# Prompt halves of the first two up tiles ahead of the sample part, and every later output-projection tile one sample later

## The reference

```
h = rms_norm(x, g_norm_mix) * (1 + scale_m) + shift_m
mla_t, dsa_t = mixer_projections(h, pos, lw)
o_mla, o_dsa = attend(mla_t, dsa_t)          # samples read 16 pages of 128 cached rows each
x = x + gate_m * (concat(rms_norm(o_mla, g_a), rms_norm(o_dsa, g_b)) @ w_out)
h = rms_norm(x, g_norm_ffn) * (1 + scale_f) + shift_f
g, u = split(h @ w_ffn_in, 2)
x = x + gate_f * ((silu(g) * u) @ w_ffn_out)
```

## Time and profile before

| | us |
|---|---|
| median of 3 runs | 1254.75 |
| lowest, highest | 1250.54, 1258.36 |
| the profiled execution, its time | 1252.33 |
| its span, first to last instruction | 1250.5 |
| PE busy | 1184.0 |
| DVE busy | 675.5 |
| ACT busy | 396.9 |

### The profile page before, as it was taken

How to read it: one execution, slowest core, us unless ns; L and a number is a source line. 1 busy time by engine, 2 the same in 40 slices (tenths; PEclk the granted TensorE clock), 3 DMA queues, 4 the chain that set the end, 5 groups by cost and what they waited for, 6 DMA issues and landing times.

```text
span 1250.5 us, 22534 instructions
## 1 busy us (share of the span) xinstructions
PE 1184.0 (95%) x9176; PEld 1060.3 (85%) x9176; DVE 675.5 (54%) x1508; ACT 396.9 (32%) x772; POOL 92.5 (7%) x138
## 2 busy tenths in 40 slices
PE   6699999998999999999999999989999999979997
PEld 4588896465687899999999888879999999959997
DVE  0643853745888787778867342342433343294330
ACT  3322333532577655555555123311001011000001
POOL 2000002001105300000000121000000000000000
PEclk9799999987999999999999999659999999999999
DMA  9597651022001202222232565302332323133321
GB/s 323 133 281 201 192 170 52 1 68 73 29 17 61 77 1 77 77 77 77 77 127 85 193 207 208 135 1 85 96 89 85 99 84 100 57 93 93 93 69 68
DMA packets 137739, 129.10 MB, mean 103 GB/s; under 512 B 17110, under 2 KB 131171, under 8 KB 135580
## 3 DMA queue, kind: packets, MB, share of 16 engines
q1 hardware_dynamic: 133596, 86.89, 23.5%
q0 software_dynamic: 4064, 41.11, 9.0%
HBM read 124.58 MB, written 3.41 MB: 102 GB/s over the span
## 4 chain that ended last, share of the span: by engine, by line
PE 82%; DVE 9%; DMA 3%; ACT 3%; issue 2%; SPq 0%; POOL 0%; DVEq 0%; ACTq 0%
PE psV L1166 19%; PE psV L950 13%; PE psA L1166 10%; PE psA L687 7%; PE psV L1062 4%; PE psV L887 2%; PE psA L1045 2%; PE psA L1113 2%; PE psA L930 2%; PE psV L911 2%; PE psV L643 2%; PE psV L749 2%; PE psA L1000 1%; PE psA L898 1%; PE psA L1036 1%
## 5 line engine op out<-in xcount | busy, mean ns | idle before, releaser
L950 PE MATMUL psV<-r_r,wide_r 128*128 128x260 f32 x1536 | 207.5, 288 | 3.3 <-DVE msk L1987 2.7
L950 PEld LDWEIGHTS psV<-r_r,wide_r 128*128 128x128 f32 x1536 | 190.4, 189 | 5.9 <-issue 3.3
L1445 ACT ACTIVATE wring<-psV 128x512 f32<-128x512 f32 x128 | 76.1, 596 | 91.5 <-PE psV L950 69.1
L1166 PE MATMUL psV<-qiz_r,wring_r 128*128 128x260 f32 x528 | 93.9, 283 | 0.0
L2183 DVE TENSOR_TENSOR wide<-wide,psV 128x520 f32 (+1 forms) x22 | 15.3, 696 | 138.4 <-PE psV L1166 138.4
L1988 DVE TENSOR_REDUCE msk<-wring 128x8 f32<-128x512 f32 x128 | 86.4, 675 | 0.0
L687 PE MATMUL psA<-wide_r,wring_r 128*128 128x260 f32 x432 | 79.8, 289 | 6.5 <-DVE hT_r L2225 6.4
L1166 PEld LDWEIGHTS psV<-qiz_r,wring_r 128*128 128x128 f32 x528 | 76.2, 188 | 0.0
L1166 PE MATMUL psA<-qiz_r,r_r 128*128 128x260 f32 x352 | 71.7, 285 | 1.6 <-DVE hT_r L2120 1.6
L1166 PE MATMUL psA<-hT_r,r_r 128*128 128x260 f32 x352 | 71.5, 285 | 0.0
L1166 PE MATMUL psA<-qiz_r,wring_r 128*128 128x260 f32 x352 | 71.4, 285 | 0.0
(11 more groups left out here) (490 smaller groups left out, 2600.2 us busy)
## 6 DMA issues: line engine op xcount, KB each, us to landing
wring<-w_ffn_in SPq DMA_DIRECT2D x44, 512.0 KB, 3.8
wide<-w_ada SPq DMA_DIRECT2D x11, 1024.0 KB, 6.8
wring<-w_ffn_out SPq DMA_DIRECT2D x16, 704.0 KB, 4.7
tok<-w_ada SPq DMA_DIRECT2D x9, 1024.0 KB, 7.6
wring<-w_in SPq DMA_DIRECT2D x24, 256.0 KB, 3.4
wring<-w_out SPq DMA_DIRECT2D x8, 512.0 KB, 8.4
wide<-w_out SPq DMA_DIRECT2D x2, 2048.0 KB, 8.3
wring<-w_in SPq DMA_DIRECT2D x20, 128.0 KB, 2.7
```

The lines of the kernel that those rows point to most:

```text
L950: mm = pe.matmul(kx[m % 2][:, hf, :], w, wtab[:, b % 2, l, 2 * k + hf, :], start=(k == 0 and w is high and l == 0), stop=(k == 1 and w is ...
L1166: mm = pe.matmul(out[:, hf, 0:HT], w[:, k, :], x[:, hf * HT:(hf + 1) * HT], start=(k0 + k == 0 and x is xh and w is high), stop=(k0 + k == ...
L1445: A(sq2[m % 2].rearrange("p (x n) -> p x n", x=2), kx[m % 2][:, :, 0:256], ACT.Square).then_inc(kx_squared, 1)
```

## The change

On PE, tile 2 moves from the open stretch to sample 1, tiles 3 to 7 to samples 2 to 6, and the sums of squares to sample 7. The first half of `sample_out` moves from ahead of `weigh_values(7)` to behind `values_out(7)`. The first two up tiles (slots 1 and 3) are split first and made in two parts: the 512 prompt columns (260 and 252) right behind `sample_out(1)`, around the small sum that the samples' DVE steps need, and the 8 sample columns when these are ready. The first two gate tiles follow whole. ACT and DVE follow: squares one sample later, the root at the start of step 6, its reciprocal inside step 7 between `row_sums` and `normalise`, all of `modulate_prompt` after step 7. DVE splits all four tiles of the first turn before the feed-forward. The two tiny matmuls go; counts are raised instead. `spm`, where `sample_out` adds up, moves to another bank.

```diff
-        spm = psA[:, 1, 1, 160:288].rearrange("p (m g b) -> p m g b", m=8, g=2)
+        spm = psA[:, 1, 0, 0:128].rearrange("p (m g b) -> p m g b", m=8, g=2)
...
+            def up_prompt(x, k0, k1):
+
+                s = 2 * x + 1
+                if k0 == 0:
+                    pe.wait_ge(w_split, 9 + x)
+                    pe.wait_ge(v_free, V_U + x - 1)
+                for k in range(k0, k1):
+                    pe.wait_ge(x_split, KD + k + 1)
+                    high, low = pieces(whigh[s])[:, k, :], pieces(wlow[s])[:, k, :]
+                    for w, xx in ((high, xhigh), (high, xlow), (low, xhigh)):
+                        for hf, c, n in ((0, 0, HT), (1, HT, SEQ - HT)):
+                            pe.matmul(sv(V_U + x)[:, hf, 0:n], w, xx[:, k, c:c + n], start=(k == 0 and w is high and xx is xhigh),
+                                      stop=(k == KD - 1 and w is low), skip_group_check=True)
+
             k_scores(0, tile=0)
             weigh(NB - 1)
-            for t in (1, 2):
-                for c4 in range(4):
-                    out_tile(t, c4)
+            for c4 in range(4):
+                out_tile(1, c4)
             pe.wait_ge(lat_out, NB)
             latent_out(NB - 1).then_inc(ol_full, 1)
-            k_scores(1, tile=3)
+            k_scores(1, tile=2)
             for b in range(NB):
                 if b >= 1:
                     values_out(b - 1)
-                if b == NB - 1:
-                    pe.wait_ge(ol_taken, 2)
-                    pe.wait_ge(wo_loaded[0], 16)
-                    for m in range(KD):
-                        sample_out(0, m)
                 weigh_values(b)
                 if b + 2 < NB:
-                    k_scores(b + 2, tile=b + 4 if b < 4 else None, sums=b == 4)
+                    k_scores(b + 2, tile=b + 3 if b < 5 else None, sums=b == 5)
...
             values_out(NB - 1)
+            pe.wait_ge(ol_taken, 2)
+            pe.wait_ge(wo_loaded[0], 16)
+            for m in range(KD):
+                sample_out(0, m)
...
             mm.then_inc(od_full, 1)
+            up_prompt(0, 0, 6)
             pe.wait_ge(s_summed, 1)
-            pe.matmul(ssum_ffn, ones, sum8, start=True, stop=True, skip_group_check=True).then_inc(a_full, 1)
+            pe.matmul(ssum_ffn, ones, sum8, start=True, stop=True, skip_group_check=True).then_inc(a_full, 1 + PADA)
+            up_prompt(0, 6, 8)
+            up_prompt(1, 0, 8)
...
             pe.wait_ge(x_split, 2 * KD + 1)
-            ffn_turn(0)
+            for x in range(2):
+                for k in range(KD):
+                    high, low = pieces(whigh[2 * x + 1])[:, k, :], pieces(wlow[2 * x + 1])[:, k, :]
+                    for w, xx in ((high, xhigh), (high, xlow), (low, xhigh)):
+                        mm = pe.matmul(sv(V_U + x)[:, 1, SEQ - HT:HT], w, xx[:, k, SEQ:T], start=(k == 0 and w is high and xx is xhigh),
+                                       stop=(k == KD - 1 and w is low), skip_group_check=True)
+                mm.then_inc(v_full, 1)
+            for x in range(2):
+                pe.wait_ge(w_split, 11 + x)
+                pe.wait_ge(a_free, A_G + x - 1)
+                passes(pieces(wlow[2 * x]), pieces(whigh[2 * x]), proj, sa(A_G + x)).then_inc(a_full, 1)
             with pe.Fori(1, KF // 2) as i:
...
             for b in range(NB - 1):
+                if b == 6:
+                    prompt_root()
                 take(NB + b)
-                if b == 5:
-                    prompt_root()
...
             A(stat[0:1, 0, 2:3], epsc[0:1], ACT.Sqrt)
-            high_part(1)
-            high_part(2)
+            high_part(0)
             take(2 * NB - 1)
...
-                elif b <= 5:
-                    add_prompt(v, b + 2)
-                elif b == NB - 1:
-                    modulate_prompt(v, 0)
+                elif b <= 6:
+                    add_prompt(v, b + 1)
                 shift(NB + b)
...
-                elif b <= 5:
-                    split_tile(v, 2, b - 4)
+                elif b == 5:
+                    split_first(v, 1, 8)
+                elif b == 6:
+                    split_first(v, 3, 9)
                 elif b == NB - 1:
-                    modulate_prompt(v, 2)
+                    v.wait_ge(v_free, V_SS2 + 1 + PADV)
+                    link(v.reciprocal(root2, root2))
                 normalise(NB + b)
...
                 if b == 6:
-                    v.wait_ge(v_free, V_SS2 + 1)
-                    link(v.reciprocal(root2, root2))
-            modulate_prompt(v, 3)
-            modulate_prompt(v, 4)
+                    split_first(v, 0, 10)
+                    split_first(v, 2, 11)
+            for k in range(3):
+                modulate_prompt(v, k)
             v.wait_ge(od_full, 1)
...
+        def split_first(v, s, n):
+
+            split(v, wraw[s], wlow[s], whigh[s], tail_w[s], 48, n)
...
-            def gate_turn(i, ahead):
+            def gate_turn(i, ahead, first=0):
 
                 for s in range(2):
-                    if s == 0 or ahead:
+                    if s >= first and (s == 0 or ahead):
...
-            with v.Fori(0, KF // 2 - 1) as i:
+            gate_turn(0, True, 1)
+            with v.Fori(1, KF // 2 - 1) as i:
```

More of the change, by code:

```diff
@@ L1074, in prompt_sums @@
                 if c4 == 3:
-                    mm.then_inc(v_full, 1)
+                    mm.then_inc(v_full, 1 + PADV)
             def k_scores(b, tile=None, sums=False):
@@ L1171, in pe_tail @@
             proj = lambda k: (xhigh[:, k, :], xlow[:, k, :])
[L1173 to L1178, removed]
             def ffn_turn(i, need=None):
@@ L1513, in prompt_root @@
             def prompt_root():
-                act.wait_ge(v_full, V_SS2 + 1)
+                act.wait_ge(v_full, V_SS2 + 1 + PADV)
                 act.wait_ge(v_free, V_SS2)
-                A(root2, psV[:, 1, 0, :], ACT.Sqrt, scale=1.0 / D, bias=epsc[:]).then_inc(v_free, 1)
+                A(root2, psV[:, 1, 0, :], ACT.Sqrt, scale=1.0 / D, bias=epsc[:]).then_inc(v_free, 1 + PADV)
             def high_part(k):
@@ L1534, in act_decode @@
             for b in range(NB - 1):
+                if b == 6:
+                    prompt_root()
                 take(NB + b)
-                if b == 5:
-                    prompt_root()
                 if b + 2 < NB:
                     take_keys(4 * b + 8)
-                else:
-                    high_part(0)
                 exps(NB + b + 1)
@@ L1544, in act_decode @@
                     take_keys(4 * b + 9)
-                if b == 4:
+                if b == 5:
                     prompt_square(6)
@@ L1550, in act_decode @@
                     take_keys(4 * b + 11)
-                if 1 <= b <= 3:
-                    prompt_square(2 * b - 2)
-                    prompt_square(2 * b - 1)
+                if 2 <= b <= 4:
+                    prompt_square(2 * b - 4)
+                    prompt_square(2 * b - 3)
             A(stat[0:1, 0, 2:3], epsc[0:1], ACT.Sqrt)
-            high_part(1)
-            high_part(2)
+            high_part(0)
             take(2 * NB - 1)
-            for k in range(3, 7):
+            for k in range(1, 6):
                 high_part(k)
+            high_part(6)
+            high_part(7)
             act.wait_ge(a_full, A_MIX + 1)
             A(rms8.rearrange("p g b -> p (g b)"), ssum_mix, ACT.Sqrt, scale=1.0 / 512, bias=epsc[:]).then_inc(a_free, 1)
-            high_part(7)
-            act.wait_ge(a_full, A_SS2 + 1)
-            A(root8, ssum_ffn, ACT.Sqrt, scale=1.0 / D, bias=epsc[:]).then_inc(a_free, 1)
+            act.wait_ge(a_full, A_SS2 + 1 + PADA)
+            A(root8, ssum_ffn, ACT.Sqrt, scale=1.0 / D, bias=epsc[:]).then_inc(a_free, 1 + PADA)
         def act_tail(act):
             A = nc.scalar.activation
-            if PADA:
-                act.wait_ge(a_full, A_SS2 + 2)
-                A(stat[0:1, 0, 0:1], sa(A_SS2 + 1)[0:1, 0, 0:1], ACT.Identity).then_inc(a_free, 1)
             with act.Fori(0, KF // 2) as i:
@@ L2080, in dve_decode @@
                 if b == 0:
-                    add_prompt(v, 2)
                     v.wait_ge(ol_full, 1)
@@ L2097, in dve_decode @@
             v.tensor_reduce(sums2[:, 1, :], sq64[:, 4:8].rearrange("p k b -> p b k"), AXX, ALU.add).then_inc(mix_s, 1)
-            modulate_prompt(v, 5)
-            modulate_prompt(v, 6)
+            for k in range(3, 8):
+                modulate_prompt(v, k)
             v.wait_ge(a_free, A_MIX + 1)
@@ L2110, in dve_decode @@
             v.tensor_reduce(sum8, sq64.rearrange("p k b -> p b k"), AXX, ALU.add).then_inc(s_summed, 1)
-            modulate_prompt(v, 7)
+            modulate_prompt(v, 8)
             link(v.tensor_tensor(hs, xs, amod[:, 1, :, 1:9], ALU.mult))
-            modulate_prompt(v, 8)
-            v.wait_ge(a_free, A_SS2 + 1)
+            v.wait_ge(a_free, A_SS2 + 1 + PADA)
             link(v.reciprocal(root8, root8))
```

5 lines of the change are left out of this document (removed).

## The result

| | before | after |
|---|---|---|
| median, us (14 runs each) | 1254.36 | 1262.74 |
| lowest, highest | 1250.54, 1258.36 | 1257.91, 1265.80 |
| profiled execution: its time | 1252.33 | 1261.52 |
| its span | 1250.5 | 1259.7 |

The ratio is 1.0067, with a 95% interval of 1.0054 to 1.008: the changed kernel is 8.4 us (0.7%) slower. 1257 had been forecast, so the sign and the range (1250 to 1265) held, and the loss is nearly four times the 2.15 us that the forecast's sum had.

A forecast was written before the change was run, and what follows sets the result against it. TensorE (PE), busy for 95% of the span, was taken to bound the kernel. The terms -2.6 - 0.35 + 3.3 + 0.1 + 1.7 gave +2.15 us, so 1257 us was forecast against the median, range 1250 to 1265.

The forecast's parts named there:

- (a): Tile 2 leaves the open stretch: sample 1's first transpose starts earlier, after a 2.7 us pause for its pages; -2.6 us.
- the clock falls in the new gaps: Rival, 22%: the clock falls at sample 1's pause or the narrow matmuls; one fall 1258.6 us, two 1260.
- (b): Sample blocks up to weigh_values(6): sample 6 carries a tile instead of the sums, sample 7 the sums; -0.35 us.
- (c): weigh_values(6) to the end of sample_out(1): sample 7's softmax loses its cover, 38.9 us for 35.67; +3.3 us.
- (d): End of sample_out(1) to the finish line: hidden 5.2 us pause paid back by 5.1 us of narrow matmuls; +0.1 us.
- (e): Start of the feed-forward loop: PE waits for its first tile's load (landing 5.3 us) and split; +1.7 us.
- two 1260: Second case of the 22% clock rival: two falls of the clock in the new gaps give 1260 us.
- A short moving operand loses the rounded rate: Rival, 12%: early up tiles' 252-column matmuls cost 0.42 us instead of 0.117, narrow ones 5.1 us more; 1277 us.
- sample_out keeps full clock: Rival, 5%: sample 7's filled block holds the clock, sample_out's instructions cost 0.106 us instead of 0.215; 1240 us.
- the clock rival: Rival, 22%: clock falls at sample 1's pause or the narrow matmuls; 1258.6 or 1260 us, 1262 to 1265 with two-instruction narrow matmuls.

The follow-up runs named there:

- so_ahead: Changed kernel with sample_out(0) put back ahead of weigh_values(7): 1258.19 us, ratio 1.0035 to the kernel before.
- narrow_inside: Changed kernel with the 48 8-column matmuls put one by one between the wide matmuls of the two gate tiles: 1257.46 us, ratio 1.004.
- shift_only: Kernel before with only tiles 2 to 7 and the sums one sample later, sample_out(0) still ahead of weigh_values(7): 1253.98 us, ratio 0.9986.
- recip_behind: Changed kernel with the root's reciprocal behind sample 7's normalising and ACT's high_part(0) behind its last take: 1262.96 us, ratio 1.0072.
- half_shift: Kernel before with tiles and sums one sample later, and first 260 columns of gate 0 and up 0 behind sample_out(1): 1249.16 us, ratio 0.9975.
- half_tiles: Kernel before with the first 260 columns of gate 0 and up 0 behind sample_out(1), no matmul added: 1250.07 and 1250.4 us, ratios 0.9965 and 0.997.
- half_between: half_tiles with gate 0 and up 0 halves between sample_out(1)'s matmuls, gate 1 and up 1 halves in the pause; output not valid: 1253.81 us, ratio 1.0003.
- early_only: Kernel before with only the early up tiles, their 48 8-column matmuls in a row, then the gates: 1258.72 us, ratio 1.0037.
- early_inside: early_only with the 48 8-column matmuls put between the wide ones of the gates: 1256.54 us, ratio 1.0016.
- gap_filled: Changed kernel with 12 unused matmuls of 512 columns in the pause ahead of sample 1's transposes: 1263.24 us, ratio 1.0077.

## Why the prediction was right and wrong

**(a) right in its term, short of its consequence.** The transpose came behind a pause of 2.69 us with a landing of 8.50, as worked out. But the clock fell behind it, and sample 1's block took 12.61 instead of 11.09 us. All six kernels with this pause that ran (the changed one, so_ahead, narrow_inside, shift_only, recip_behind, half_shift) show a first quarter tile of 2.1 to 2.5 us there, and the one with the pause filled shows 1.40. I had this as a rival at 22% ("the clock falls in the new gaps") and as part of no sum; it belonged in the sum. The Trainium skill (TensorE: Matmul & The Clock Gate, HAM oscillation) describes a loop in which PE waits some 3 to 5 us for a DMA between short bursts, and says that each burst starts cold. Here it did six times of six, after waits of 2.67 to 3.05 us, at or under the short end of what the page describes.

**(b) the price of the blocks held, and falls of the clock came on top.** weigh_values(4) to (6) took 29.50 us for a forecast of 26.3. The difference is two falls of the clock, seen as 1.48 at 768.67 and 1.87 at 782.73. Each makes its block 1.6 us longer. That the first belongs to the change isn't shown: the two profiles of half_tiles, the same code, have three falls and one in the samples' blocks; half_between has one, and early_only and early_inside, which leave PE's work in the blocks as it was, have three each. The profile of before, with one, was a lucky one to build on. The second looks like more than chance, though the numbers are small. The block with the sums of squares took 15.4 us in all six profiles of kernels with the pause of (a) (in so_ahead 783.93 to 799.37), where it takes 13.8 at full clock; it took 13.8 in gap_filled, and in the six kernels with the old order 13.8 four times and 15.4 twice. Why it is hit stays open: gap_filled is one profile. One fall more in the last phase of the kernel (112.61 us for 924 matmuls, 111.08 before) may be chance too.

**(c) right in the trace, wrong in what it was compared with.** 38.57 for a forecast of 38.9 (3.2 over before, which the prediction wrote as 3.3), with the pause of 5.47 where 5.6 was forecast. The shift by itself shortens this stretch from 35.67 to 33.98 (so_ahead), 34.09 (half_shift) and 34.50 (shift_only), so the new place of sample_out(0) costs 4.1 to 4.6 us in the traces, and 4.0 in the medians. The stretch's sum held because I had worked out the whole stretch and not the part.

**(d) the step that failed.** Prompt parts: 13.7 for a forecast of 13.6, and 252 columns cost about what 260 cost (60 matmuls of both kinds in 7.17 us, 0.119 each). Narrow ones: 5.96 for 5.1. Gate 0: 8.27 for 5.77. The term took the price of the narrow matmuls from rows at full clock and asked nothing of the clock behind them. It fell in their last 1.6 us and stayed at half for the first 5.2 us of gate 0: 3.3 us, the largest single miss of this profile. It fell there in all five profiles with the narrow matmuls in a row, but its cost varies: narrow matmuls and gate 0 together, 10.9 by forecast, took 14.2 here and in recip_behind, and 12.6 to 12.7 in so_ahead, gap_filled and early_only. narrow_inside shows the fall by its absence. The price at full clock was right: the Trainium skill's rule for a weight load (same page, LDWEIGHTS; columns divided by 1.2 GHz, 107 ns here) agrees with the 0.11 us between starts. The 25 ns that the page gives (Back-to-back issue gap) is a floor for the matmul alone, and not the price of these.

**(e) too high by 1.1.** The loop waited 0.56 us, not 1.7, because the load landed in 4.04 us and not in 5.3; the median of 3.8 was the better of the two rows.

**The rivals.** "The clock falls in the new gaps" is what happened, at both of the places that it names, on top of the forecast rather than beside it; its second case, "two 1260", is 2.7 us under what was measured, and nearer than 1257. "A short moving operand loses the rounded rate" is refuted (252 columns at about the 260-column price; by the prediction's own rows the unsplit operands are 3.6 times as dear, not 3.7). "sample_out keeps full clock" is refuted: the window from 800 has 0.51, and the 96 matmuls took 20.58 us, 0.214 each.

**The sum.** +2.15 forecast; +1.5 behind the pause, +3.3 in (d) and -1.1 in (e) make +5.9; the two falls in (b) (+3.2) and the -0.4 of (c) bring it to +8.6, against 8.75 in the profile. So the finish line came at 871.00 and not at 864 to 866. The medians' 8.4 is less well explained than that profile. Over the five profiles the fall in (d) cost 2.4 us on average and not 3.3, and of (b) only the fall in the block with the sums, at most 1.6, came back with the shifted order: 2.15 + 1.5 + 2.4 - 1.1 - 0.4 + 1.6 = 6.2. The remaining 2 us have no place that a run here has shown. The experiments on the parts leave 1.6 open (6.8 of 8.4). The 8.4 has an interval of 6.8 to 10.0 and each part one of about 3 either way, so the remainder may be nothing.

The range held, the sum did not: it put every fall of the clock at nothing, and the loss came out at about four times its size. What kept the time inside was the width, 8 us above the forecast, left for the clock rival with its 22%; and the wait in (e), put too high by 1.1, hid a part of the miss. That is some luck on top of a sound list of places.

## What to carry to other kernels

To hide a pause of PE, move whole matmuls that are wanted anyway: splitting a product so that its last 8 columns come later turns them into matmuls that cost a weight load each, and 48 of those cost the 5 us that the pause did. When a new stretch of narrow matmuls or a new pause of some microseconds is costed, and the traces at hand show such falls, add the fall of the clock behind it to the sum, not to the rivals, and count it in the work that follows. When a part's cover is moved, work out the stretch with and without the cover, not against the old kernel: its neighbours move too.

## What the hardware showed that I had not expected

- A pause of 2.7 to 3.1 us, in front of a block with wide matmuls, was enough to lose the full clock in six of six profiles; 2.9 us of matmuls in its place kept it (one profile).
- 48 matmuls of 8 columns, one each 0.11 us, with PE busy for all of the time, ended at half clock in five of five profiles; the fall cost 1.8 us in three of them and 3.3 in two. The same 48 between pairs of 260-column matmuls did not lose it (narrow_inside, early_inside).
- Once the clock is at half, wide matmuls one by one between narrow ones did not bring it back in over 20 us with PE always busy (half_between), where wide matmuls in a row did: some 2 us into the row behind that mixture, and in the changed kernel 5.2 us into gate 0.
- The same code has one fall of the clock in the samples' blocks in one profile and three in another, 1.4 to 1.6 us each, with PE busy. The block with the sums had a fall in six of six profiles with the pause ahead of sample 1, and in two of six with the old order. A difference of 3 us between two profiles is no finding before the medians show it.
